# Hybrid attention / matrix-memory trunk on one core: matrix memory interleaved head by head, its first gates and blocks during attention, the last head by token halves amid the transposes, and a reordered start

## The reference, cut to what matters

```
def mixer(hx, hc, cos, sin, p, need_ctx_out):
    ...
    a_x = blocked_attention(q_x, k_all, v_all)
    ...
    m_x, m_c = mlstm_bidirectional(lat, ctm, need_ctx_out)
    y_x = merge_groups(a_x, m_x, o_x, p)

def merge_groups(a, hm, o, p):
    b, t, _ = o.shape
    hm = jnp.swapaxes(hm, 1, 2) * jax.nn.sigmoid(o.astype(jnp.float32)).reshape(b, t, MLSTM_HEADS, MLSTM_DH)
    hm = head_layer_norm(hm, p['mlstm_norm']).astype(a.dtype)
    return jnp.concatenate([rms_norm(a, p['attn_out_norm']), hm], axis=-1) @ p['w_out']
```

## Time and profile before

| | us |
|---|---|
| median of 3 runs | 3213.77 (3212.32 to 3216.13) |
| the profiled execution: its own time | 3212.62 |
| its span in the profile | 3210.7 |
| PE busy | 3016.6 (94%) |
| DVE busy | 1700.6 (53%) |
| ACT busy | 1019.5 (32%) |
| POOL busy | 264.6 (8%) |
| mean granted clock of PE | 0.964 |

### The profile page before, as it was taken

One profiled execution on the slowest core, in us unless ns is written; L12 is line 12 of the kernel. 1 busy time (PEld: TensorE's weight loads), 2 busy tenths in 40 slices (PEclk: granted clock), 3 DMA queues, 4 the chain that ended last, 5 costly groups with the idle time before them and its releaser, 6 DMA issues. The chain is left out here.

```text
span 3210.7 us, 49435 instructions
## 1 busy us (share of the span) xinstructions
PE 3016.6 (94%) x18100; PEld 2835.2 (88%) x18100; DVE 1700.6 (53%) x3013; ACT 1019.5 (32%) x1720; POOL 264.6 (8%) x215
## 2 busy tenths in 40 slices
PE   6999999989898799999999999999998898899998
PEld 5999999979775689999999899999978665899997
DVE  4566566555246763455326575445555347643334
ACT  3212112443434452121224312212343434532233
POOL 1000000410000050000005000000320000400002
PEclk7999999999998899999999999999999998999999
DMA  6444344322100032244323344325332100423333
GB/s 205 120 136 130 106 131 130 107 76 59 56 1 1 27 106 64 87 118 118 85 66 113 111 124 131 98 86 143 99 89 66 57 1 1 126 86 98 92 92 112
DMA packets 454132, 293.21 MB, mean 91 GB/s; under 512 B 25974, under 2 KB 411356, under 8 KB 453980
## 3 DMA queue, kind: packets, MB, share of 16 engines
q1 hardware_dynamic: 453456, 291.01, 31.3%
q10 hardware_dynamic: 524, 0.18, 0.0%
HBM read 289.04 MB, written 2.10 MB: 91 GB/s over the span
## 5 line engine op out<-in xcount | busy, mean ns | idle before, releaser
L1683 PE MATMUL ps<-hn,wsp 128*128 128x384 f32 (+1 forms) x3200 | 1052.6, 329 | 39.5 <-DVE hn L1250 18.4
L1684 PE MATMUL ps<-hn,wsp 128*128 128x384 f32 (+1 forms) x3200 | 1043.8, 326 | 0.0
L1685 PE MATMUL ps<-hn,wsp 128*128 128x384 f32 (+1 forms) x3200 | 1043.7, 326 | 0.0
L1162 DVE TENSOR_TENSOR wsp<-raw,wsp 128x1024 fp32r<-128x1024 f32 x370 | 459.0, 1241 | 509.2 <-ACT wsp L782 508.8
L1683 PEld LDWEIGHTS ps<-hn,wsp 128*128 128x128 f32 x3200 | 610.7, 191 | 54.0 <-issue 33.0
L1684 PEld LDWEIGHTS ps<-hn,wsp 128*128 128x128 f32 x3200 | 611.5, 191 | 0.0
L1685 PEld LDWEIGHTS ps<-hn,wsp 128*128 128x128 f32 x3200 | 610.9, 191 | 0.0
L782 ACT ACTIVATE wsp<-raw 128x1024 fp32r<-128x1024 f32 x408 | 429.1, 1052 | 516.8 <-PE ps L1685 516.7
L1683 PE MATMUL ps<-aT,wsp 128*128 128x384 f32 (+1 forms) x1408 | 460.1, 327 | 23.2 <-DVE aT L1341 19.3
L1684 PE MATMUL ps<-aT,wsp 128*128 128x384 f32 (+1 forms) x1408 | 456.0, 324 | 0.0
L1685 PE MATMUL ps<-aT,wsp 128*128 128x384 f32 (+1 forms) x1408 | 455.8, 324 | 0.0
(11 more groups left out here) (209 smaller groups left out, 2953.2 us busy)
## 6 DMA issues: line engine op xcount, KB each, us to landing
modw<-in_w_mod SPq DMA_DIRECT2D x144, 512.0 KB, 4.2
raw<-in_ffn_w_gate SPq DMA_DIRECT2D x192, 256.0 KB, 3.4
raw<-in_ffn_w_up SPq DMA_DIRECT2D x192, 256.0 KB, 4.2
raw<-in_ffn_w_down SPq DMA_DIRECT2D x64, 448.0 KB, 3.3
raw<-in_w_in SPq DMA_DIRECT2D x96, 256.0 KB, 3.0
raw<-in_ffn_w_down SPq DMA_DIRECT2D x64, 256.0 KB, 4.2
raw<-in_w_out SPq DMA_DIRECT2D x64, 256.0 KB, 3.2
raw<-in_ffn_w_down SPq DMA_DIRECT2D x64, 192.0 KB, 3.4
```

What stands on the lines that cost most here:

```text
L1162: dve.tensor_tensor(wsp[:, cs, 1, 0:width], raw[:, slot, 0:width], wsp[:, cs, 0, 0:width].bitcast(F32), ALU.subtract).then_inc(wlo_done, 1)
L1683: pe.matmul(dst, w(0), x(0), start=first, stop=False)
L1684: pe.matmul(dst, w(0), x(1), start=False, stop=False)
L1685: return pe.matmul(dst, w(1), x(0), start=False, stop=last)
```

## The change

In the memory part:

- The gates of head 0 are spread ahead of the first attention scores, and ACT makes the decays of its first two source tiles during the last seven attention items.
- `dbuf` is replaced by three pairs of buffers (`dbuf3`, the two new pairs lie over buffers that attention has finished with), and `gbc` by two.
- The masked diagonal goes from DVE to POOL, as a plain addition of gate and mask; the column bias is added in ACT's exponential, as for the rest.
- PE runs one unit of head h-1's `head_out` after each of the scores 1 to 4 of head h, and the gates of head h+1 behind scores 3 and 5. DVE runs one unit of `mlstm_out` after each of the blocks 0 to 3. That function has three operations on a few columns where it had four, and for d = 1 it multiplies and adds in one operation for each token tile.
- The product with the output gate goes to POOL (`merge`) for heads 0 to 2, the normalisation to POOL (heads 0, 1) and ACT (heads 2, 3). Means and variances follow two heads later, inside the block loop, as do the attention rows' squares and their scaling on ACT.
- The last head's units are taken by token half, and PE's transposes, ACT's and DVE's splits stand between them.

At the start:

- `mod_first(0)` runs between the two halves of the token transposes and `mod_first(1)` right after the second half, ahead of the first mean. The mean and spread of token half 1 move into the first weight tile's products.
- POOL makes the low parts of the first two weight tiles.
- The table `FIRST` puts weight splits 2 and 3 between the normalisation steps of token half 1.

```diff
 FIRST = {
-    "DVE": [("split",)] + [("pre", 0, k) for k in PAIRS] + [("head", 0), ("head", 1)]
-           + [("pre", 1, k) for k in PAIRS] + [("head", 2), ("head", 3)],
...
-    "POOL": [],
-    "PE": {},
+    "DVE": [("pre", 0, 0), ("pre", 0, 2), ("pre", 0, 4), ("root", 1), ("pre", 0, 6), ("pre", 1, 0), ("head", 0),
+            ("pre", 1, 2), ("head", 1), ("pre", 1, 4), ("pre", 1, 6), ("head", 2), ("head", 3)],
...
+    "POOL": [("split",)],
+    "PE": {(0, 3): ("mean", 0, 1), (0, 7): ("spread", 0, 1)},
 }
...
+            def matrix_memory(l):
+                tts = o_tts(l)
+                for h in range(MH):
+                    for j in range(NT):
+                        for d in range(2):
...
+                            pool.tensor_tensor(
+                                dbuf3[j % 3][d][:, s], gbc2[h % 2][:, d, s], cst[:, C_MF + d * P:C_MF + (d + 1) * P], ALU.add
+                            ).then_inc(dg_done, 1)
+                        if h >= 2 and j == 0:
+                            merge(l, h - 2)
+                        if h == MH - 1 and j == NT - 2:
+                            fin(l, 0)
+                merge(l, MH - 2)
+                fin(l, 1)
...
+                gates_out_of(0, 0)
+                gates_out_of(0, 1)
+                ahead = {len(items) - 7 + 2 * i: (i // 2, i % 2) for i in range(4)}
                 for i in range(len(items) + 1):
                     if i < len(items):
                         attn_exp(i)
                     if i >= 1:
                         pt_evac(i - 1)
+                    if i in ahead:
+                        decays(0, *ahead[i])
...
+                for h in range(MH):
+                    for j in range(NT):
                         for d in range(2):
...
+                            products(h, j, d)
+                        if h >= 1 and j < 4:
+                            mlstm_out(l, h - 1, j)
+                        if h >= 2 and 1 <= j <= 3:
+                            moments(h - 2, tts[2 * (j - 1):2 * j])
...
+                last = MH - 1
+                mlstm_out(l, last, 0)
+                moments(last - 1, tts)
...
+                mlstm_out(l, last, 1)
+                gated(last, 0)
+                moments(last, triples(l)[0])
...
+                mlstm_out(l, last, 2)
+                mlstm_out(l, last, 3)
+                gated(last, 1)
+                mix_lo(0, 7)
...
+                for h in range(MH):
+                    for j in range(NT):
+                        source_scores(h, j)
...
+                        if h >= 1 and 1 <= j <= 4:
+                            head_out(h - 1, j - 1)
+                        if h + 1 < MH and j in (3, 5):
+                            spread_gate(h + 1, j // 4)
+                head_out(last, 0)
+                pe.wait_ge(pb_done, block_index(l, last, NT, 0))
+                mix_turns(0, range(HEADS))
+                head_out(last, 1)
+                mix_turns(0, range(HEADS, KD - 1))
+                head_out(last, 2)
+                head_out(last, 3)
+                mix_turns(0, [KD - 1])
+                mix_turns(1, range(KD))
...
+            x_turns(0)
             pe.wait_ge(silz_done, 2)
+            mod_first(0)
+            x_turns(1)
+            mod_first(1)
             pe.wait_ge(xev, 2 * KD)
-            mod_first(0)
+            mod0_turn(0)
             mean(0, 0, 0, 0)
```

## The result

The changed kernel takes **3165.6 us** (median of 4 runs, 3163.8 to 3172.6) against 3213.9 for the kernel before, run beside it (3212.3 to 3216.1). The ratio is 0.9854, with a 95% interval of 0.9838 to 0.9869: 48 us faster, where 64 were forecast. The profiled execution took 3166.6 us with a span of 3164.8.

What follows compares the result with a forecast made beforehand. The prediction saw a chain at the start and, in the memory stages, PE and DVE waiting for each other, neither full. 3212.6 - 13 (start) - 29.7 (layer 0) - 21.5 (layer 1) = 3148.4, 3149 with the median's offset; range 3128 to 3172.

Steps and rivals of the forecast that it cites:

- (a): Start: with root and split off DVE's path, normalisation starts right after the columns; 3.8 us saved.
- (b): Start: earlier `mod_first` calls free the ring buffers sooner, so the last conditioning piece lands about 4 us earlier.
- (d): Start: PE's 5.0 us wait for weight tile 4 shrinks to about 1, as splits 2 and 3 come earlier.
- (c): Start: mean and spread inside the first weight tile cost PE about 1.5 us.
- (e): Start: PE no longer runs at the lower clock again after the wait for weight tile 4; roughly 2 us saved.
- Layer 0, clock 2: Layer 0, end of attention to first output product: 2 us added for PE's clock, since PE has gaps.
- Head 3, 19 and 15.4 forecast: Last head's period: in layer 0, DVE's 16 us plus a wait of some 3, 19; in layer 1, 15.4.
- The gates ahead of attention: Head 0's gates partly fill PE's wait for rotated queries; attention starts 1.5 us late in layer 0, 2.5 in layer 1.
- The tail, 27 and 20.5: After the last head: DVE's 22.6 us plus 4 for handoffs and waits, 27, in layer 0; 20.5 in layer 1.
- POOL holds DVE: Rival: POOL's 7 us a head (5 in layer 1) and its tail all add to DVE's; about 3190 us, chance 0.08.
- Handoffs eat half: Rival: block handoffs between PE and DVE make middle heads 24 us in layer 0, 20 in layer 1; about 3168, chance 0.14.
- PE stays at its lower level: Rival: PE's work from attention to the output product all at 1.2 GHz, 162 and 137 us; about 3266, chance 0.04.

Runs made afterwards that it cites:

- run 5: The change with head 0's eight gate products moved into PE's wait ahead of the second pair of rotary products; 3149.8 us against 3165.4 for the change.
- Run 3: The change with the normalisation of heads 0 and 1 on ACT instead of POOL; 3172.3 us.
- Run 11: The change with head 0's gates in PE's wait, head 1's inverse deviation formed earlier and three filling products in head 0 of layer 0; 3148.4 us.
- run 4: The change with the 80 mask additions to the diagonals on DVE instead of POOL; 3184.2 us.
- run 10: The change with its tail in blocks: the last head's four output groups first, then all sixteen transposes, on PE and DVE; 3176.6 us.
- runs 9: The change with head 0's gates in PE's wait, plus DVE's inverse deviation of head 1 formed earlier; 3149.8 us against 3151.7 without the earlier inverse.

## Why the prediction was right, and where it was off

The mechanism and the side were right, the size was too large: 3149 forecast, 3166 measured, inside 3128 to 3172. PE's scores wait 4.6 us for DVE's blocks in layer 0 where they waited 14.2, and DVE has 16.5 us of work in a head of 22.3. No run takes the units of `head_out` back out from between the scores, so what that step gives by itself is read from these waits and not from a time. By its own steps:

- **The start, 13 forecast:** 11.7 in the changed kernel's trace, 14.2 and 10.3 (median) alone. PE's first network product comes 6.7 us earlier, against 3.8 + 4 of (a) and (b): the last piece was used 3.9 us earlier, as (b) said, and behind it DVE lost 0.7 us waiting for POOL (last section) and 0.9 for ACT. From there to the first down product it is 113.9 us instead of 118.3 (157.8 - 43.9 and 168.9 - 50.6), 4.4 less. Of that (d) is 4.6, for 4; mean and spread in the first tile took 1.27 and 1.48, 2.8 for the 1.5 of (c), as the clock is 0.50 there until 59 us; by difference some 2.5 is left for (e).
- **PE's and DVE's work for a head:** right. With the clock at 1.00, heads 1 and 2 of layer 0 take 18.9 and 20.4 to 20.5 (19 and 20.5 forecast), and heads 1 and 2 of layer 1 16.6 and 16.5 (16.8 and 17). Head 0 of layer 0 takes 11.5 for 10.
- **Layer 0, clock 2:** this is the term that was mis-sized. In the first trace heads 0 and 1 take 16.9 and 21.8 for 11.5 and 18.9 without the fall: 8.3 us in two heads. I had put 2 for the layer. The fall is in five of the six traces with the gates behind the wait and head 0 unfilled; that two waits of 0.60 and 1.13 are followed by it in one execution and not in another is shown by the change's two traces. What decides it stays open. In layer 1 the same term, also 2, was mis-sized by less: the last head takes 20.9 us with the fall and 17.9 without (run 5, whose tail is 1.4 longer).
- **Head 3, 19 and 15.4 forecast:** 22.3 in layer 0 and 20.9 in layer 1 (2648.1 to 2669.0, of which ten at a clock of 0.66; that costs the 3.0 us above). My sum took DVE's 16 us and PE's 19 and left ACT out, which has 17.6 of the 22.3 us in layer 0: the scaling of `atok` and the table loads come on top of the decays. The head begins with ACT late by a root and a table load, and DVE's first products wait for its decays:

```profile
1020.06 1.28 ACT L1141 ACT_TABLE_LOAD   x1
1021.35 0.40 ACT L1141 ACTIVATE krT<-krT,colF 128x128 f32<-128x128 f32 x1
1021.79 0.29 DVE L1666 SCALAR_TENSOR_TENSOR pblkE<-ps,krT 128x128 f32<-128x128 f32 x1 [1.25 <-ACT krT L1141]
1024.53 1.81 DVE L1666 SCALAR_TENSOR_TENSOR pblkO<-ps,dbuf 128x256 f32<-128x256 f32 x4 [0.93 <-ACT dbuf L1141]
```

These 2.2 us are what the trace shows of ACT pacing the head; that it accounts for the whole 3.3 is argued. Run 3 shows that POOL's normalisations don't.
- **The gates ahead of attention, late by 1.5 and 2.5:** 1.7 to 4.3 in layer 0 and 4.7 in layer 1. I had assumed that they partly fill PE's wait for the rotated queries. They stood behind it. Run 5 moved them into it: 5.2 and 7.4 us of the layers' sums came back, against the change in the same set, though 1.7 of the latter lie in C to O, where the clock of the last head rose.
- **Attention itself, forecast unchanged:** 89.6 and 77.2 for 88.2 and 76.6, some 2 us in both layers with the decays and POOL's additions beside it. Run 11 had 88.3 and 76.1, with a clock of 1.00 and 0.98 where the change had 0.98 and 0.96, so part of it is clock. Not settled.
- **The tail, 27 and 20.5:** 27.5 to 28.4 and 18.7. The total is right in layer 0 and 1.8 too large in layer 1, but by luck: I had put 4 us for handoffs in layer 0, and the waits for POOL, ACT and `mixL` add to 9.0 us there and to 6.8 in layer 1.

Of the signs named, five came: PE's first product at 43.9, no 5 us wait, 48 + 32 additions at 0.46, heads some 20 and 17 us apart, products within 0.69. C to O of 95 to 100 us in layer 0 did not (108.9), and layer 1 stands just above its 77 to 82. All three things that I had said would prove it wrong came too: the clock of 0.67 in head 0, PE waiting for DVE more than 3 us in a head (4.5 in head 3, of which 2.9 at its end), and the waits for POOL's and ACT's normalisation (2.7 and 1.9). By its own words, then, the account of the heads was wrong in these places, and the time stayed in the range only because the range had room for them. *POOL holds DVE* is out as a whole: the middle heads take the forecast periods with POOL's additions in them, and run 4 shows the additions dearer on DVE. It is true of single operations (last section). *Handoffs eat half* gave nearly the right time (3168) for the wrong reason, as the middle heads take the forecast periods. *PE stays at its lower level* happened for some 17 us in the heads, and the clock of C to O as a whole rose in layer 1 (0.94 for 0.82) and stayed at 0.87 in layer 0. That rival's own sum was also off: twice 78 and twice 66 are 156 and 132 us, not 162 and 137.

The sum for the change: 45.1 = 11.7 + 16.9 + 16.6 (rounded), and the missing 19 of the 64: start 1.3, layer 0 12.8 (heads 0 and 1 9.7, head 3 3.3, attention 1.4, tail 0.5, less 2 allowed for the clock), layer 1 4.9 (gates 2.2, attention 0.6, C to O 2.1). The spans differ by 45.9, so 0.8 of the 19 came back outside these marks.

## What to carry to other kernels

Short work that is pulled forward belongs inside a wait, not behind it: eight products of 36 rows cost 5.5 us behind a wait and nothing measurable in it, and the 13 to 16 us between the medians of the two placements are about a third of what the whole change gave. Read one stage from several executions before explaining it by the change: heads 0 and 1 differed by 8 us between two traces of one kernel whose times agreed within 1.3 us. And a bound for a head needs all three engines: the one that was left out of the sum, ACT, held up DVE at the start of head 3 and was as full as PE there (17.6 and 17.8 us).

## What the runs showed of the hardware

**The lower level moves about.** The granted clock fell to 0.50 (1.2 GHz) in head 0 after gaps of 1.13 and 0.60 us in some executions (16.9 us for the head in the change's first trace, 17.0 in runs 3 and 10) and stayed at 1.00 (2.4 GHz) in another of the same kernel with the same gaps (11.5). Where it stayed, other stretches had it. The same is seen in the last head of layer 1: 10 us at 0.66 in the change, 1.00 in run 10 with the same instructions up to there.

**A small DVE operation can wait out POOL's.** DVE and POOL in head 3 of the change:

```profile
1039.46 1.80 POOL L818 TENSOR_TENSOR otok<-otok,hh 128x768 f32<-128x768 f32 x1 [4.11 <-DVE hh L1783]
...
1039.77 0.29 DVE L1676 BATCH_NORM_STATS2 bn<-otok 128x6 f32<-128x128 f32 x1
1040.32 0.97 DVE L1681 COPY stat<-mv 128x6 f32<-128x6 f32 x1
```

The copy of six columns takes 0.97 us instead of 0.17 and ends at 1041.29, when POOL's merge ends (1041.26); the statistics of 128 columns beside the same merge keep their 0.29. At the start the same is seen: `gcol` (L1343) takes 0.86 instead of 0.17 and ends at 40.47, POOL's addition at 40.44.

```profile
39.41 1.03 POOL L743 TENSOR_TENSOR scr<-scr 128x384 f32<-128x384 f32 x1 [2.83 <-ACT scr L880]
39.61 0.86 DVE L1343 SCALAR_TENSOR_TENSOR gcol<-colt,vecA 128x16 f32<-128x16 f32 x1
```

The same copy takes 0.97 or 0.98 us beside this merge in every trace of a kernel with the new memory part, and `gcol` 0.86 to 0.92 in every one with the new start; alone, both take 0.16 to 0.18. Four additions of run 4 do the same.

By the rule weighed in the prediction (the Trainium skill, SBUF — State Buffer, section "SBUF: two separate sides"), an exclusive lock contended by operations of two SBUF inputs or a two-port mode, `gcol` with its two SBUF inputs has to wait and the products with one operand in PSUM do not; this trace agrees in both. But not every operation of POOL holds DVE for its whole time. Beside POOL's normalisation of 128 columns (0.79 us) the same copy took 0.18 to 0.23 us in runs 9, 10 and 11, and two additions of run 4, with two SBUF inputs, kept their 0.28:

```profile
1026.19 4.05 POOL L796 TENSOR_SCALAR otok<-otok,mv,stat 128x128 f32<-128x128 f32 x5 [4.65 <-DVE stat L1702]
1027.60 0.28 DVE L1680 TENSOR_TENSOR scr<-gbc,cst 128x128 f32<-128x128 f32 x1
1028.60 0.28 DVE L1680 TENSOR_TENSOR scr<-gbc,cst 128x128 f32<-128x128 f32 x1
```

Which property of the POOL operation decides, no run here shows. In the change the wait cost 0.7 and 0.8 us, at two places of its path.
